# A recurrent mixer's convolution split between VectorE and GpSimd, with its two norms in the other order

## The chip, the cores and the metric

The kernel runs on one core of a Trainium2 chip. The metric is the device time of one execution in microseconds. Five engines take part: TensorE (PE, with its weight loads shown as PEld), VectorE (DVE), ScalarE (ACT), GpSimd (POOL) and SyncE (SP), which issues the loads.

## The reference

The program runs two model blocks one after the other on 512 tokens of width 1024. The part that matters here is the mixer of the first layer, `mixer_ab`: a recurrence over the tokens (RWKV-7, eight heads of 64) beside a causal depthwise convolution of 31 taps over 512 channels.

```python
y = rwkv7_scan(rh, hs(decay), kh, vh, kk, hs(a))
mu = jnp.mean(y, axis=-1, keepdims=True)                 # group norm: per head
yc = y - mu
y = yc * lax.rsqrt(jnp.mean(yc * yc, axis=-1, keepdims=True) + GN_EPS)
y = y.reshape(b, t, D_RWKV) * lnx_g + lnx_b
bonus = jnp.sum(rh * kh * r_k, axis=-1, keepdims=True) * vh
y_a = (y + bonus.reshape(b, t, D_RWKV)) * g
glu = c_val * jax.nn.sigmoid(c_gate)
conv = lax.conv_general_dilated(glu, conv_w[:, None, :], window_strides=(1,),
    padding=[(CONV_WIDTH - 1, 0)], dimension_numbers=('NWC', 'WIO', 'NWC'),
    feature_group_count=D_CONV) + conv_b                 # CONV_WIDTH = 31
y_b = jax.nn.silu(layer_norm(conv, conv_ln_g, conv_ln_b, CONV_LN_EPS))
return jnp.concatenate([y_a, y_b], axis=-1) @ w_out      # x = x + rms_norm(that, g[3])
```

All data is float32. Everything else (four plain feed-forward parts, an attention mixer, two hybrid mixers, two cross attentions, two gated feed-forward parts) is untouched by the change, apart from line numbers.

## The kernel before

Activations lie features by tokens: a tile is 128 features (partitions) by 512 tokens, so the mixer's output is 8 tiles: tiles 0 to 3 of `H` hold the recurrent half, tiles 4 to 7 the convolution half. Each large product splits both operands into a rounded part and a remainder and runs three matmuls for each pair of tiles (L245, L246, L254): ScalarE rounds (`WHI`, `WK_R`), VectorE subtracts (`WLO`, `H_LO`).

The code is one instruction stream for each engine, written out by hand; semaphores order the streams. Nothing is scheduled by a planner: an engine does its instructions in the order of its stream, and a wait holds everything behind it.

The mixer (`make_mixa`) runs like this. TensorE makes 22 panels of the input projection; VectorE scales each (L2507, L2509), shifts it (L2514) and makes the factors of the recurrence. `factors_made` counts these; it reaches 24 when `rho_made` (L2460) is done, and from then on the tiles of `e_in` are free, in whose place the convolution's sums `acc` lie. Then VectorE inverts 32 by 32 triangles (L2529, L2530: 31 steps of two small instructions, each waiting for the last), masks two Gram matrices out of PSUM (L2474, `masked`), and runs the convolution.

The convolution is 31 taps on 4 tiles. A tap is one VectorE instruction on a 128 by 512 tile, `acc = glu shifted by j * weight + acc` (L2490, with `glu` and `acc` both in SBUF; the first tap of a tile is a `tensor_scalar`, L2487). The list runs over all tiles for tap 0, then tap 1 and so on. `conv(n)` puts the next n of the 124 into VectorE's stream. They fill places where VectorE would wait:

- `conv(68)` ahead of the four additions into `rho` (L2537), which wait for TensorE's first four rounds of `tokens` (L2248);
- `conv(20)` ahead of the scan;
- `conv(1)` in each of the scan's 14 steps;
- `conv(6)` and the last 16 after the scan, between instructions of the group norm.

The scan goes over chunks of 32 tokens. In each step VectorE makes a decayed state `d` (L2544, L2545), takes one tap, and adds TensorE's product out of PSUM (L2551, two halves); TensorE then makes the next product (L2266) and the step's outputs (L2271).

After the scan ScalarE copies `y` out of PSUM (L2365). The group norm follows: sums by head (L2276), centring (L2554), squares (L2368), their sums (L2113), root and reciprocal (L2371, L2557), spread back to the tiles (L2120), then three VectorE instructions for each of 4 tiles (L2565 to L2567). The layer norm of the convolution needs all taps: sums over channels (L2285), centring (L2562), squares (L2374), sums (L2290), root (L2377), reciprocal (L2569), spread (L2295), product (L2572), SiLU (L2380). Then `parts_act` and `parts_dve` split the 8 tiles, 0 to 7, and the output product takes them in that order, tile by tile in its first panel.

GpSimd does almost nothing in the mixer: one DMA for the small weights and three memsets.

Of the kernel before, what the change touches and what calls it, by code (L numbers as in the profile page):

```python
# [27 lines left out]
ALU = mybir.AluOpType  # L28
# [6 lines left out]
T = 512  # L35
# [5 lines left out]
HD = 64  # L41
# [49 lines left out]
def build(nc, dram, out, phases, final=True):  # L91
    ctx = ExitStack()
    with ctx:
# [142 lines left out]
        def feature_hi(pe, p, s_, hi, ks, first, i=0, n=T, fresh=None):  # L236


            slot = p.nslot(s_)
            pe.wait_ge(S("w_lo"), p.N + (s_ + 1))  # L240
            for b_, k in enumerate(ks):
                w, o = slice(128 * b_, 128 * b_ + 128), PS[:, 4 * p.slot + i, 0:n]
                if fresh:
                    pe.wait_ge(S(fresh[0]), fresh[2] + k + 1)
                pe.matmul(o, WHI[:, slot, w], hi(k), start=(first and b_ == 0), stop=False)  # L245
                pe.matmul(o, WLO[:, slot, w], hi(k), start=False, stop=False)  # L246

        def feature_lo(pe, p, s_, lo, ks, last, i=0, n=T, fresh=None):

            for b_, k in enumerate(ks):  # L250
                w, o = slice(128 * b_, 128 * b_ + 128), PS[:, 4 * p.slot + i, 0:n]
                if fresh:
                    pe.wait_ge(S(fresh[1]), fresh[2] + k + 1)
                mm = pe.matmul(o, WHI[:, p.nslot(s_), w], lo(k), start=False, stop=(last and b_ == len(ks) - 1))  # L254
            mm.then_inc(S("piece_done"), 1)
# [1779 lines left out]
def make_mixa(env):  # L2035
# [31 lines left out]
    KKB, LORA = [1, 2, 3, 5], [6, 7]  # L2067

# [18 lines left out]
    def pool(pool, idx, n, b):  # L2087
        pool.wait_ge(S("norm_sum"), b["norm"] + 1)
        pool.dma_start(SC[:, 2:4, :], env["dram"]["a_lora"].rearrange("p (a c) -> p a c", a=2)).then_inc(S("lora_loaded"), 16)
        nc.gpsimd.memset(glu[:, :, 0:PAD], 0.0).then_inc(S("pool_set"), 1)  # L2090
        pool.wait_ge(S("glu_made"), 4)
        nc.gpsimd.memset(Tp, 0.0).then_inc(S("pool_set"), 1)
        pool.wait_ge(S("pool_set"), 2)
        nc.gpsimd.memset(flat(HID, 16, 1024)[:, 0:1024:C + 1], 1.0).then_inc(S("pool_set"), 1)

    def pe(pe, idx, n, b):
# [176 lines left out]

        for f in range(4):
            pe.wait_ge(S("y_copied"), f + 1)
            pe.matmul(PS[:, BA[f], :], blk, y[:, f, :], start=True, stop=True).then_inc(S("gn_sums"), 1)  # L2276
        for f in range(4):
            pe.wait_ge(S("head_squares"), 4 + f + 1)
            head_sums(f, BB[f], SC[:, 4:8, :], "gn_sums")
        pe.wait_ge(S("head_recips"), 2)  # L2280
        for f in range(4):
            head_spread(f, BA[f], "gn_sums")
        pe.wait_ge(S("conv_tap"), 4 * CONVW)
        for f in range(4):
            mm = pe.matmul(PS[:, BB[0], :], ones, acc[:, f, :], start=(f == 0), stop=(f == 3))  # L2285
        mm.then_inc(S("gn_sums"), 1)
        for f in range(4):
            pe.wait_ge(S("head_squares"), 8 + f + 1)
            for t in range(TT):
                mm = pe.matmul(PS[:, BB[1], 128 * t:128 * t + 128], csq[:, f, 128 * t:128 * t + 128], ones, start=(f == 0 and t == 0),  # L2290
                               stop=(f == 3 and t == TT - 1))
        mm.then_inc(S("gn_sums"), 1)
        pe.wait_ge(S("head_recips"), 3)
        for t in range(TT):
            mm = pe.matmul(PS[:, BB[2], 128 * t:128 * t + 128], recips[:, t:t + 1].to_broadcast([128, 128]), ident, start=True, stop=True)  # L2295
        mm.then_inc(S("gn_sums"), 1)

    def act(act, idx, n, b):
# [85 lines left out]
        env["parts_act"](act, made, b["mix"], DT, HI0)  # L2384

    def dve(dve, idx, n, b):
# [90 lines left out]
        taps = [(j, f) for j in range(CONVW) for f in range(4)]  # L2477
        done = [0]

        def conv(count):  # L2480

            for _ in range(min(count, len(taps) - done[0])):
# [5 lines left out]
                else:  # L2488
                    dve.wait_ge(S("conv_tap"), done[0] - 3)
# [44 lines left out]
        conv(68)  # L2534
# [3 lines left out]
        conv(20)  # L2538
        dve.wait_ge(S("ef_copied"), 16)
        for c in range(1, NCH - 1):  # L2540
# [7 lines left out]
            for par in range(2):  # L2548
                rows = slice(64 * par, 64 * par + 64)
                f_s = PS[rows, BA[2 * (c % 2) + par], 0:256].rearrange("p (h v) -> p h v", h=NHP)  # L2550
                tt(state(c + 1)[rows], d[rows], f_s, ALU.add).then_inc(S("state_ready"), 1)  # L2551
        for f in range(4):
            dve.wait_ge(S("gn_sums"), f + 1)
            stt(out=y[:, f, :], in0=PS[:, BA[f], :], scalar=-1.0 / HD, in1=y[:, f, :], op0=ALU.mult, op1=ALU.add).then_inc(S("centred"), 1)  # L2554
# [4 lines left out]
        dve.wait_ge(S("conv_tap"), 4 * CONVW)  # L2559
        dve.wait_ge(S("gn_sums"), 13)  # L2560
        for f in range(4):
            stt(out=acc[:, f, :], in0=PS[:, BB[0], :], scalar=-1.0 / 512, in1=acc[:, f, :], op0=ALU.mult, op1=ALU.add).then_inc(S("centred"), 1)  # L2562
        for f in range(4):
            dve.wait_ge(S("gn_sums"), 8 + f + 1)
            st.done(stt(out=y[:, f, :], in0=y[:, f, :], scalar=vec("lnx_g", f), in1=PS[:, BA[f], :], op0=ALU.mult, op1=ALU.mult))  # L2565
            st.done(stt(out=y[:, f, :], in0=y[:, f, :], scalar=vec("lnx_b", f), in1=bonus[:, f, :], op0=ALU.add, op1=ALU.add))
            tt(H[:, f, :], y[:, f, :], G_[:, f, :], ALU.mult).then_inc(S("rwkv_out"), 1)  # L2567
        dve.wait_ge(S("head_roots"), 6)
        ve.reciprocal(recips[:, 0:TT], sums[:, 0:TT]).then_inc(S("head_recips"), 1)  # L2569
        dve.wait_ge(S("gn_sums"), 15)  # L2570
        for f in range(4):
            tt(acc[:, f, :], acc[:, f, :], PS[:, BB[2], :], ALU.mult).then_inc(S("ln_normed"), 1)  # L2572
        env["parts_dve"](dve, b["mix"], DT, HI0)
# [129 lines left out]
```

## Time and profile before

| what | before |
|---|---|
| median of 3 runs | 3728.59 us (3719.97 to 3729.72) |
| the profiled execution | 3726.07 us, its span 3724.3 us |
| TensorE busy | 95% of the span |
| VectorE busy | 53% |
| ScalarE busy | 40% |
| GpSimd busy | 20.6 us, 1% |
| mean granted TensorE clock | 0.975 of full speed |

In the page's 40 slices of the span TensorE is busy nine tenths or more nearly everywhere, except in slices 6 to 8, about 560 to 750 us: the recurrence, its scan and the two norms. There TensorE's granted clock also falls. A stage bound by TensorE gives nothing when another engine gets faster; this stretch is where VectorE and the waits between the engines set the time. How the rows are read: a timeline row gives start, length, engine, line, operation, output and inputs with shapes, and in brackets the engine's idle time ahead of it with who ended it. A row of the chain of waits gives a piece of the path that ended last.

### The profile page before, as it was taken

What the parts mean: (1) busy time and instruction counts of PE and PEld (TensorE: products, weight loads), DVE (VectorE), ACT (ScalarE), POOL (GpSimd) and SP (SyncE); (2) the same over time, 40 slices, a digit from 0 to 9 for tenths busy, and PEclk for the clock granted to TensorE, in tenths of its full rate; (3) what the DMA queues carried; (4) which work ended last, traced back from release to release, by engine and by line L of the source; (5) the groups of instructions that cost most, each with busy time, mean ns of one, the idle gap of its engine ahead of it and who ended that gap; (6) DMA issues with size and microseconds to landing.
All of it is one profiled execution on the core that took longest, in us unless ns stands there. A gap on an engine that the chain in (4) does not pass through costs nothing.

```text
span 3724.3 us, 55194 instructions
## 1 busy us (share of the span) xinstructions
PE 3544.7 (95%) x21764; PEld 2954.4 (79%) x21764; DVE 1961.6 (53%) x2712; ACT 1473.7 (40%) x2212; POOL 20.6 (1%) x38
## 2 busy tenths in 40 slices
PE   7999996699999999999999999999999998989998
PEld 6888775578887888898678888778788896778887
DVE  3442469844434443325744433755677357566753
ACT  3332432143323332334643323655444237454432
POOL 0000000000000000000000000000000000000000
PEclk9999996699999999999999999999999999999999
DMA  3223220012232223222022233102222330222232
GB/s 114 96 94 99 78 69 15 2 63 96 96 95 81 96 97 95 85 91 85 7 79 96 96 94 95 38 29 86 91 96 94 99 101 13 68 80 90 96 94 92
DMA packets 84100, 296.11 MB, mean 80 GB/s; under 512 B 9504, under 2 KB 9504, under 8 KB 83680
## 3 DMA queue, kind: packets, MB, share of 16 engines
q1 hardware_dynamic: 82512, 288.24, 24.5%
q0 software_dynamic: 1424, 5.51, 0.4%
q8 instruction: 124, 2.03, 0.2%
q14 instruction: 40, 0.33, 0.0%
HBM read 291.61 MB, written 2.10 MB: 79 GB/s over the span
## 4 chain that ended last, share of the span: by engine, by line
PE 89%; DVE 6%; ACT 2%; issue 2%; DMA 1%; SPq 0%; DVEq 0%; ACTq 0%
PE PS L254 22%; PE PS L245 22%; PE PS L246 22%; PE PS L331 2%; PE PS L334 2%; PE PS L332 2%; PE PS L365 2%; PE PS L937 2%; PE PS L948 1%; PE PS L961 1%; PE PS L277 1%; DVE H_LO L438 1%; PE PS L278 1%; ACT WHI L217 1%; DVE WLO L221 1%
## 5 line engine op out<-in xcount | busy, mean ns | idle before, releaser
L245 PE MATMUL PS<-WK_R,WHI 128*128 128x512 f32 (+1 forms) x3680 | 1430.4, 389 | 13.6 <-ACT WK_R L585 6.9
L246 PE MATMUL PS<-WK_R,WLO 128*128 128x512 f32 (+1 forms) x3680 | 1425.5, 388 | 0.0
L221 DVE TENSOR_TENSOR WLO<-RAW,WHI 128x1024 fp32r<-128x1024 f32 x563 | 689.1, 1225 | 1211.9 <-ACT WHI L217 1209.2
L217 ACT ACTIVATE WHI<-RAW 128x1024 fp32r<-128x1024 f32 x563 | 596.0, 1059 | 995.0 <-PE PS L254 820.7
L245 PEld LDWEIGHTS PS<-WK_R,WHI 128*128 128x128 f32 x3680 | 692.8, 188 | 164.9 <-issue 19.6
L246 PEld LDWEIGHTS PS<-WK_R,WLO 128*128 128x128 f32 x3680 | 692.8, 188 | 141.0 <-issue 0.7
L254 PE MATMUL PS<-H_LO,WHI 128*128 128x512 f32 x2680 | 674.4, 391 | 4.7 <-DVE H_LO L438 4.3
L254 PEld LDWEIGHTS PS<-H_LO,WHI 128*128 128x128 f32 x2680 | 501.9, 188 | 118.6 <-DVE H_LO L438 16.4
L254 PE MATMUL PS<-HID_LO,WHI 128*128 128x512 f32 x1056 | 263.2, 389 | 0.0
L254 PEld LDWEIGHTS PS<-HID_LO,WHI 128*128 128x128 f32 x1056 | 197.9, 188 | 40.9
L1129 DVE SCALAR_TENSOR_TENSOR SC<-SC,VEC 128x511 f32<-128x511 f32 x176 | 132.2, 751 | 110.5 <-ACT SC L1096 98.6
L331 PE MATMUL PS<-WHI,WK_R 128*128 128x256 f32 (+1 forms) x608 | 159.2, 293 | 1.6 <-DVE WLO L221 1.6
L613 ACT ACTIVATE WK_R<-HID (+1 forms) x88 | 55.6, 632 | 260.9 <-DVE HID L630 260.9
L332 PE MATMUL PS<-WLO,WK_R 128*128 128x256 f32 (+1 forms) x608 | 158.8, 292 | 0.0
L1096 ACT ACTIVATE SC<-SC,VEC 128x512 f32<-128x512 f32 x88 | 71.8, 816 | 178.9 <-DVE SC L1119 178.9
L610 ACT ACTIVATE SC<-SC 128x512 f32<-128x512 f32 x88 | 55.7, 632 | 159.4 <-DVE SC L624 158.9
L331 PEld LDWEIGHTS PS<-WHI,WK_R 128*128 128x128 f32 x608 | 115.9, 191 | 2.1 <-issue 1.8
L332 PEld LDWEIGHTS PS<-WLO,WK_R 128*128 128x128 f32 x608 | 116.0, 191 | 0.0
L632 DVE TENSOR_TENSOR HID_LO<-HID,WK_R (+1 forms) x88 | 60.9, 693 | 86.7 <-ACT WK_R L613 86.7
L1010 DVE TENSOR_REDUCE AS<-PS 128x2 f32<-128x1024 f32 (+2 forms) x80 | 85.1, 1064 | 32.6 <-PE PS L937 31.1
L365 PEld LDWEIGHTS PS<-CON,SC 128*128 128x128 f32 x640 | 82.4, 193 | 17.8 <-ACT SC L515 6.7
L365 PE MATMUL PS<-CON,SC 128*128 128x128 f32 x640 | 86.0, 279 | 7.8 <-ACT SC L515 4.1
(375 smaller groups left out, 3526.0 us busy)
## 6 DMA issues: line engine op xcount, KB each, us to landing
RAW<-in_ffn_gu SPq DMA_DIRECT2D x176, 512.0 KB, 3.5
RAW<-in_f_up SPq DMA_DIRECT2D x88, 512.0 KB, 3.6
RAW<-in_ffn_dn SPq DMA_DIRECT2D x64, 512.0 KB, 3.5
RAW<-in_c_in SPq DMA_DIRECT2D x32, 512.0 KB, 3.5
RAW<-in_f_dn SPq DMA_DIRECT2D x32, 512.0 KB, 3.5
RAW<-in_ffn_dn SPq DMA_DIRECT2D x32, 384.0 KB, 3.1
RAW<-in_a_in SPq DMA_DIRECT2D x22, 512.0 KB, 3.4
RAW<-in_b_out SPq DMA_DIRECT2D x16, 512.0 KB, 3.6
```

The source lines that it names most:

```text
L217: nc.scalar.activation(WHI[:, slot, :], RAW[:, slot, :], ACT.Copy).then_inc(S("w_hi"), 1)
L221: nc.vector.tensor_tensor(WLO[:, slot, :], RAW[:, slot, :], WHI[:, slot, :].bitcast(F32), ALU.subtract).then_inc(S("w_lo"), 1)
L245: pe.matmul(o, WHI[:, slot, w], hi(k), start=(first and b_ == 0), stop=False)
L246: pe.matmul(o, WLO[:, slot, w], hi(k), start=False, stop=False)
L254: mm = pe.matmul(o, WHI[:, p.nslot(s_), w], lo(k), start=False, stop=(last and b_ == len(ks) - 1))
L331: pe.matmul(o, hi(k, t), WHI[:, slot, w], start=(first and b_ == 0), stop=False)
L332: pe.matmul(o, hi(k, t), WLO[:, slot, w], start=False, stop=False)
L334: mm = pe.matmul(o, lo(k, t), WHI[:, slot, w], start=False, stop=(last and b_ == len(ks) - 1))
L365: mm = pe.matmul(PS[:, b_, 128 * t:128 * t + 128], SC[:, k, 128 * t:128 * t + 128], ones, start=(first and t == 0), stop=(last and t == TT ...
L937: mm = pe.matmul(PS[:, score_banks(u).start + i, 0:n], q, k_, start=(k == 0), stop=(k == len(products) - 1))
L1010: nc.vector.reduce_max(stat(1, U), PS[:, banks, 0:n], AX.X, negate=True).then_inc(S("at_max"), 1)
L1129: nc.vector.scalar_tensor_tensor(out=o, in0=s, scalar=vec("fcw", (idx * 3 + tap) * 2 * FT + part * FT + e), in1=o, op0=ALU.mult, op1=ALU.a ...
```

## The change

It has four parts, all in the mixer or in helpers that only the mixer uses differently.

1. **GpSimd makes tile 3 of the convolution.** Once `factors_made` reaches 24, it runs 31 taps as two instructions each: a product of the shifted `glu` with the weight (broadcast along the tokens) into a spare tile `WK[:, 29]`, and an addition to `acc[:, 3]`. Each waits for the one before by the semaphore `conv_pool`: 62 instructions of 128 by 512, all inputs in SBUF.
2. **VectorE's 93 taps** (3 tiles) all stand ahead of the scan: `conv(62)` ahead of the additions into `rho`, `conv(31)` behind them. The `conv(1)` in the scan's steps finds nothing left.
3. **Layer norm ahead of group norm.** Behind the scan TensorE sums `acc` over channels first, then the head sums of `y`, and so on; the two norms alternate. Banks of PSUM are dealt out anew for that.
4. **Output tiles in the order 4 to 7, 0 to 3.** ScalarE and VectorE split the convolution half first, and the output product takes its tiles in that order (in each of its 8 panels).

The core of the diff:

```diff
@@ feature_hi, feature_lo
-                w, o = slice(128 * b_, 128 * b_ + 128), PS[:, 4 * p.slot + i, 0:n]
+                w, o = slice(128 * (k % 8), 128 * (k % 8) + 128), PS[:, 4 * p.slot + i, 0:n]
@@ out_pieces
+            if kind == "mixa":
+                return [[4, 5, 6, 7, 0, 1, 2, 3]]
@@ make_mixa
+    OUT_ORDER = (4, 5, 6, 7, 0, 1, 2, 3)
+    OWN = 3
+    SPREAD = [BA[1], BA[2], BA[3], BB[3]]
@@ pool
+        pool.wait_ge(S("factors_made"), 24)
+        part, o = WK[:, 29, :], acc[:, OWN, :]
+        for j in range(CONVW):
+            w = vec("cw", 4 * j + OWN).to_broadcast([128, T])
+            if j > 0:
+                pool.wait_ge(S("conv_pool"), 2 * j)
+            nc.gpsimd.tensor_tensor(part, glu[:, OWN, j:j + T], w, ALU.mult).then_inc(S("conv_pool"), 1)
+            pool.wait_ge(S("conv_pool"), 2 * j + 1)
+            before = vec("cb", OWN).to_broadcast([128, T]) if j == 0 else o
+            nc.gpsimd.tensor_tensor(o, part, before, ALU.add).then_inc(S("conv_pool"), 1)
@@ pe, behind the scan
+        pe.wait_ge(S("conv_tap"), 3 * CONVW)
+        pe.wait_ge(S("conv_pool"), 2 * CONVW)
+        for f in range(4):
+            mm = pe.matmul(PS[:, BA[0], :], ones, acc[:, f, :], start=(f == 0), stop=(f == 3))
+        mm.then_inc(S("ln_sums"), 1)
...
+        pe.wait_ge(S("ln_recip"), 1)
...
         pe.wait_ge(S("head_recips"), 2)
         for f in range(4):
-            head_spread(f, BA[f], "gn_sums")
-        pe.wait_ge(S("conv_tap"), 4 * CONVW)
...
+            head_spread(f, SPREAD[f], "gn_sums")
@@ dve
-        taps = [(j, f) for j in range(CONVW) for f in range(4)]
+        taps = [(j, f) for j in range(CONVW) for f in range(OWN)]
...
-        conv(68)
+        conv(62)
...
-        conv(20)
+        conv(31)
...
-        conv(6)
+        dve.wait_ge(S("ln_root"), 1)
+        ve.reciprocal(recips[:, 0:TT], sums[:, 0:TT]).then_inc(S("ln_recip"), 1)
+        dve.wait_ge(S("ln_sums"), 3)
+        for f in range(4):
+            tt(acc[:, f, :], acc[:, f, :], PS[:, BA[0], :], ALU.mult).then_inc(S("ln_normed"), 1)
         dve.wait_ge(S("head_roots"), 5)
         ve.reciprocal(recips, sums).then_inc(S("head_recips"), 1)
-        conv(len(taps))
...
```

How the streams change at the places the prediction speaks of. VectorE from the end of the inverse into the scan, before (L2490 is a tap, L2537 the additions into `rho`, L2551 the state):

```order
L2531 STREAM_TRANSPOSE SC<-HID 128x32x32
L2474 TENSOR_TENSOR HID<-PS,CON 128x512 x4
L2487 TENSOR_SCALAR WK<-WK,VEC 128x512 x4
L2490 SCALAR_TENSOR_TENSOR WK<-WK,VEC 128x512 x64
L2537 TENSOR_TENSOR HID<-HID,PS 128x512 x4
L2490 SCALAR_TENSOR_TENSOR WK<-WK,VEC 128x512 x20
L2544 TENSOR_TENSOR RS<-H,ST 128x256
L2545 TENSOR_TENSOR RS<-RS,H 128x256
L2490 SCALAR_TENSOR_TENSOR WK<-WK,VEC 128x512
L2551 TENSOR_TENSOR WK<-RS,PS 64x256 x2
```

VectorE at the same place in the changed kernel (L2506 is a tap, L2553 the additions, L2567 the state):

```order
L2547 STREAM_TRANSPOSE SC<-HID 128x32x32
L2490 TENSOR_TENSOR HID<-PS,CON 128x512 x4
L2503 TENSOR_SCALAR WK<-WK,VEC 128x512 x3
L2506 SCALAR_TENSOR_TENSOR WK<-WK,VEC 128x512 x59
L2553 TENSOR_TENSOR HID<-HID,PS 128x512 x4
L2506 SCALAR_TENSOR_TENSOR WK<-WK,VEC 128x512 x31
L2560 TENSOR_TENSOR RS<-H,ST 128x256
L2561 TENSOR_TENSOR RS<-RS,H 128x256
L2567 TENSOR_TENSOR WK<-RS,PS 64x256 x2
```

Six fewer taps ahead of the additions, eleven more behind them, none between the scan's instructions.

TensorE behind the scan, before (L2276, L2113, L2120 group norm; L2285, L2290, L2295 layer norm; L245 the output product):

```order
L2271 MATMUL PS<-HID 64x32 x16
L2276 MATMUL PS<-WK,CON 128x512 x4
L2113 MATMUL PS<-CON,SC 128x128 x16
L2120 MATMUL PS<-CON,ST 64x128 x32
L2285 MATMUL PS<-WK,CON 128x512 x4
L2290 MATMUL PS<-CON,WK 128x128 x16
L2295 MATMUL PS<-CON,ST 128x128 x4
```

And in the changed kernel (L2292, L2300, L2308 layer norm; L2296, L2128, L2135 group norm):

```order
L2286 MATMUL PS<-HID 64x32 x16
L2292 MATMUL PS<-WK,CON 128x512 x4
L2296 MATMUL PS<-WK,CON 128x512 x4
L2300 MATMUL PS<-CON,WK 128x128 x16
L2128 MATMUL PS<-CON,SC 128x128 x16
L2308 MATMUL PS<-CON,ST 128x128 x4
L2135 MATMUL PS<-CON,ST 64x128 x32
```

Each step of the layer norm now stands ahead of a step of the group norm; the instructions are the same in number and kind.

GpSimd in the changed kernel, behind its last memset of the mixer (the pair L2106, L2109 comes 31 times):

```order
L2099 MEMSET HID 128x32 [waits pool_set]
L2106 ISA
L2106 TENSOR_TENSOR WK<-WK,VEC 128x512 [waits factors_made]
L2109 TENSOR_TENSOR WK<-WK,VEC 128x512 [waits conv_pool]
L2106 TENSOR_TENSOR WK<-WK,VEC 128x512 [waits conv_pool]
L2109 TENSOR_TENSOR WK<-WK 128x512 [waits conv_pool]
```

GpSimd's next instruction before the change, the loads of the first hybrid mixer, comes more than a millisecond later.

## Rows read from the trace of the kernel before

**Rows 1.** The page's first line.

```profile
span 3724.3 us, 55194 instructions
```

**Rows 2.** Timeline of VectorE, 575 to 703 us: start, length, engine, line, operation.

```profile
575.13 0.19 DVE L2529 TENSOR_TENSOR RS<-SC,HID 128x31 f32<-128x31 f32 x1
...
604.51 42.49 DVE L2490 SCALAR_TENSOR_TENSOR WK<-WK,VEC 128x512 f32<-128x512 f32 x64
649.61 2.48 DVE L2537 TENSOR_TENSOR HID<-HID,PS 128x512 f32<-128x512 f32 x4 [2.61 <-PE PS L2248]
...
668.34 0.87 DVE L2551 TENSOR_TENSOR WK<-RS,PS 64x256 f32<-64x256 f32 x2 [1.41 <-PE PS L2266]
669.24 0.42 DVE L2544 TENSOR_TENSOR RS<-WK,ST 128x256 f32<-128x256 f32 x1
...
702.22 0.87 DVE L2551 TENSOR_TENSOR HID<-RS,PS 64x256 f32<-64x256 f32 x2
```

**Rows 3.** Timeline of TensorE, the scan's first two products.

```profile
667.17 1.12 PE L2266 MATMUL PS<-H,WK 64*64 64x64 f32 x16
...
669.26 1.12 PE L2266 MATMUL PS<-WK 64*64 64x64 f32 x16 [0.17 <-DVE WK L2551]
```

**Rows 4.** Chain of waits, 703 to 751 us: start, length, piece.

```profile
704.91 6.66 PE PS L2276 x8
...
716.52 10.52 DVE WK L2490 x16
...
735.49 0.67 DVE WK L2565
...
747.15 2.93 ACT H L2380 x4
...
750.74 0.77 PE PS L245
```

**Rows 5.** Timeline of TensorE, sums and spreads of the two norms.

```profile
716.57 3.71 PE L2120 MATMUL PS<-CON,ST 128*64 128x128 f32 x64 [1.45 <-DVE ST L2557]
...
734.41 3.84 PE L2290 MATMUL PS<-CON,WK 128*128 128x128 f32 x32 [1.52 <-ACT WK L2374]
744.31 2.07 PE L2295 MATMUL PS<-CON,ST 128*128 128x128 f32 x8 [6.06 <-DVE ST L2569]
```

**Rows 6.** Timeline of ScalarE: rounding the mixer's output; first panel done.

```profile
749.98 4.25 ACT L585 ACTIVATE WK_R<-H 128x512 fp32r<-128x512 f32 x8
758.60 0.60 ACT L515 ACTIVATE SC<-PS 128x512 f32<-128x512 f32 x1 [4.37 <-PE PS L254]
```

**Rows 7.** Busy time by stretch: window, length, then by engine; PEclk is the granted clock.

```profile
751.00:755.20 4.20, 4.20 (x11) 3.24 (x11) 4.20 (x8) 3.23 (x7) 0.00 (x0) 0.50 0.02 4
```

**Rows 8.** Timeline of GpSimd, one of its six additions (in a hybrid mixer).

```profile
2427.43 1.27 POOL L1645 TENSOR_TENSOR HID<-HID 128x512 f32<-128x512 f32 x1 [135.85 <-ACT HID L1883]
```

**Rows 9.** Timeline of VectorE around that addition, and one round later.

```profile
2426.75 1.22 DVE L1010 TENSOR_REDUCE AS<-PS 128x2 f32<-128x1024 f32 x1
...
2428.08 1.30 DVE L1019 TENSOR_SCALAR SC<-SC,AS 128x512 f32<-128x512 f32 x2
...
2433.54 1.22 DVE L1010 TENSOR_REDUCE AS<-PS 128x2 f32<-128x1024 f32 x1 [1.27 <-PE PS L937]
...
2434.87 0.88 DVE L1019 TENSOR_SCALAR SC<-SC,AS 128x512 f32<-128x512 f32 x2
```

**Rows 10.** Timelines of VectorE and TensorE, 549 to 568 us.

```profile
549.90 2.49 DVE L2460 TENSOR_TENSOR HID<-HID,WK 128x512 f32<-128x512 f32 x4
...
557.06 1.23 DVE L221 TENSOR_TENSOR WLO<-RAW,WHI 128x1024 fp32r<-128x1024 f32 x1 [4.02 <-ACT WHI L217]
...
562.50 1.22 DVE L221 TENSOR_TENSOR WLO<-RAW,WHI 128x1024 fp32r<-128x1024 f32 x1 [0.54 <-ACT WHI L217]
...
567.45 2.65 PE L2133 MATMUL PS<-WK,HID 64*32 64x32 f32 x186 [6.13 <-DVE HID L2514]
```

**Rows 11.** Busy time by stretch, VectorE alone: the small instructions of the inverse.

```profile
575.10:598.50 23.40, 21.27 (x62) 0.72 0.02 4
```

More of the change, by code:

```diff
@@ L2272, in pe @@
         mm.then_inc(S("y_done"), 1)
+        pe.wait_ge(S("conv_tap"), 3 * CONVW)
[3 more added lines that the diff above has]
+        mm.then_inc(S("ln_sums"), 1)
         for f in range(4):
             pe.wait_ge(S("y_copied"), f + 1)
-            pe.matmul(PS[:, BA[f], :], blk, y[:, f, :], start=True, stop=True).then_inc(S("gn_sums"), 1)
+            pe.matmul(PS[:, BB[f], :], blk, y[:, f, :], start=True, stop=True).then_inc(S("gn_sums"), 1)
+        for f in range(4):
+            pe.wait_ge(S("ln_squares"), f + 1)
+            for t in range(TT):
+                mm = pe.matmul(PS[:, BA[1], 128 * t:128 * t + 128], csq[:, f, 128 * t:128 * t + 128], ones, start=(f == 0 and t == 0),
+                               stop=(f == 3 and t == TT - 1))
+        mm.then_inc(S("ln_sums"), 1)
         for f in range(4):
@@ L2279, in pe @@
             head_sums(f, BB[f], SC[:, 4:8, :], "gn_sums")
+        pe.wait_ge(S("ln_recip"), 1)
+        for t in range(TT):
+            mm = pe.matmul(PS[:, BA[0], 128 * t:128 * t + 128], recips[:, t:t + 1].to_broadcast([128, 128]), ident, start=True, stop=True)
+        mm.then_inc(S("ln_sums"), 1)
         pe.wait_ge(S("head_recips"), 2)
         for f in range(4):
-            head_spread(f, BA[f], "gn_sums")
-        pe.wait_ge(S("conv_tap"), 4 * CONVW)
[L2284 to L2296, printed above, removed]
+            head_spread(f, SPREAD[f], "gn_sums")
     def act(act, idx, n, b):
@@ L2366, in act @@
         for f in range(4):
+            act.wait_ge(S("ln_centred"), f + 1)
+            sc.activation(csq[:, f, :], acc[:, f, :], ACT.Square).then_inc(S("ln_squares"), 1)
+        for f in range(4):
             act.wait_ge(S("centred"), f + 1)
             sc.activation(SC[:, 4 + f, :], y[:, f, :], ACT.Square).then_inc(S("head_squares"), 1)
+        act.wait_ge(S("ln_sums"), 2)
+        sc.activation(sums[:, 0:TT], PS[:, BA[1], 0:T:128], ACT.Sqrt, bias=eps[:, 3:4], scale=1.0 / 512).then_inc(S("ln_root"), 1)
+        act.wait_ge(S("ln_recip"), 1)
         for f in range(4):
@@ L2488, in conv @@
                 else:
-                    dve.wait_ge(S("conv_tap"), done[0] - 3)
+                    dve.wait_ge(S("conv_tap"), done[0] - 2)
                     i = stt(out=acc[:, f, :], in0=src, scalar=w, in1=acc[:, f, :], op0=ALU.mult, op1=ALU.add)
@@ L2551, in dve @@
                 tt(state(c + 1)[rows], d[rows], f_s, ALU.add).then_inc(S("state_ready"), 1)
+        assert done[0] == len(taps)
+        dve.wait_ge(S("ln_sums"), 1)
+        dve.wait_ge(S("conv_tap"), len(taps))
+        dve.wait_ge(S("conv_pool"), 2 * CONVW)
+        for f in range(4):
+            stt(out=acc[:, f, :], in0=PS[:, BA[0], :], scalar=-1.0 / 512, in1=acc[:, f, :], op0=ALU.mult, op1=ALU.add).then_inc(S("ln_centred"), 1)
         for f in range(4):
             dve.wait_ge(S("gn_sums"), f + 1)
-            stt(out=y[:, f, :], in0=PS[:, BA[f], :], scalar=-1.0 / HD, in1=y[:, f, :], op0=ALU.mult, op1=ALU.add).then_inc(S("centred"), 1)
@@ L2559, in dve @@
[L2559 to L2562, printed above, removed]
         for f in range(4):
             dve.wait_ge(S("gn_sums"), 8 + f + 1)
-            st.done(stt(out=y[:, f, :], in0=y[:, f, :], scalar=vec("lnx_g", f), in1=PS[:, BA[f], :], op0=ALU.mult, op1=ALU.mult))
+            st.done(stt(out=y[:, f, :], in0=y[:, f, :], scalar=vec("lnx_g", f), in1=PS[:, SPREAD[f], :], op0=ALU.mult, op1=ALU.mult))
```

33 lines of the change are left out of this document (12 added, 21 removed).

## The prediction

> **What bounds the kernel now.** I read the page first: the profiled execution spans 3724.3 us [rows 1] of its 3726.1, and TensorE is busy in 95% of it. Only the mixer of the first layer, some 190 us, is not TensorE's. There I read the timelines of VectorE and TensorE side by side, then the chain of waits. What the reader is to see:
>
> Ahead of the scan both engines are close to level. VectorE's 64 taps take 42.49 us, 0.664 each; then it waits 2.61 us for TensorE before the additions into `rho`, which end at 652.1 [rows 2]. At the scan's first state it waits 1.41 us for TensorE.
>
> In the scan VectorE is the bound: its states come from 668.34 to 702.22, 13 periods of 2.606 us, without a gap [rows 2]. The one period in which TensorE had the last word is the first: from product to product 2.09 us [rows 3]. So a tap costs the scan about 0.52 us a step.
>
> Behind the scan everything hangs in one chain: head sums, centring, group norm's sums, 16 taps in a row (10.52 us), the layer norm's sums, the twelve instructions of the group norm (from 735.49, about 8.7 us), spread, SiLU, and only then TensorE's output product at 750.74 [rows 4]. Its first panel is done at 758.6 [rows 6]. From the last state (703.1) that is 55.5 us.
>
> **The change, part by part.** All times are set against the profiled execution's 3726.1 us, 2.5 below the median.
>
> *Taps ahead of the scan.* 3 tensor_scalars and 59 taps are shorter than what stood there, so without any disturbance the `rho` additions still wait for TensorE and end at 652.1. Behind them stand 31 taps: 31 x 0.664 = 20.6, to 672.7, plus two small ones (0.46 each): the first state comes at 673.6, not 668.3: **+5.3 us**.
>
> *The scan.* 13 periods of 2.09 for 2.606 [rows 2, 3]: **-6.7 us**. Its last state is then ready at 701.7: 1.4 us earlier in all. What is late next in the scan is TensorE's product.
>
> *Behind the scan.* Call the last state's end 0. Before, the first output panel is done at 55.5. Now:
> - The layer norm's sums need no copy of `y` and start at about 1.1; four products of 128 by 512 took 6.66 at the low clock [rows 4]: 7.8.
> - The head sums of `y` follow directly. The engine has then been busy without a break, and in the profile the sums behind a busy stretch run faster; bounds 3.3 (half of 6.66, twice the clock) and 6.66, I take 4: 11.8.
> - Sums of the layer norm's squares, 3.8: 15.6. Sums of the group norm's squares, as many matmuls of the same size, 3.7: 19.3 [rows 5]. ScalarE's and VectorE's parts run beside them.
> - The layer norm's spread, 1 to 2.1 [rows 5], say 1.6: 20.9. Its four products on VectorE 2.5 (as four instructions with one PSUM input in [rows 2]): 23.4; SiLU (2.93, [rows 4]) and rounding are beside that.
> - The group norm's reciprocal stands behind these four; its spread takes 3.7 [rows 5]. VectorE's twelve instructions begin after a quarter of it, about 24.7, and last 8.7: 33.4. TensorE starts the output product at about 27.4 with tiles 4 to 7 and then waits for tiles 0 to 3.
> - Eight remainders `H_LO` of about 0.61 on VectorE stand behind the twelve: 38.3. They were hidden before (VectorE idle during SiLU) and are now last: TensorE's third part follows them. Panel done at 38.5.
>
> So **-17.0 us**. The output product's start at the low clock (0.50 in its first 4.2 us, [rows 7]) was paid before as well; broken up as it now is, it may be paid again in the second panel: 0 to +2.2, I take **+1.9**.
>
> Sum of these: 5.3 - 6.7 - 17.0 + 1.9 = -16.5, that is 3709.6, if GpSimd's 62 instructions cost nobody anything.
>
> *GpSimd's instructions.* An addition of 128 by 512 takes 1.27 us [rows 8]. They start when `rho_made` is done, 552.3 [rows 10]; 62 x about 1.33 = 82 us, to 635, far ahead of the scan's end. So GpSimd's own time is hidden, as long as nobody disturbs it.
>
> *Whom they disturb.* Two rows decide here. While GpSimd's addition ran (from 2427.43), VectorE issued a pair of tensor_scalars, SBUF to SBUF, at 2428.08, and they took 1.30 us; the same pair one round later took 0.88 [rows 9]. All four places in the trace where the two meet look like this. So VectorE was held 0.42 us, until 1.07 us after GpSimd's start. The reduction out of PSUM that also overlapped took the usual 1.22 [rows 9]. I read this as: a running GpSimd tensor_tensor keeps something of SBUF's for about 1.07 us of its 1.27, and VectorE's SBUF work waits for it whole. No row shows a VectorE instruction with two SBUF inputs beside GpSimd. The bounds are no hold at all (as for the PSUM reader) and a hold by the whole of GpSimd's instruction. I take the hold of 1.07, since a tap and the inverse's instructions take both inputs from SBUF and write to it, and are thus nearer to the tensor_scalar than to the reduction.
>
> Then each of GpSimd's 62 instructions costs VectorE 1.07 less the 0.15 or so of its own instruction that needs no data (a tap of 0.664 has 512 columns; the inverse's smallest, 31 columns, still takes 0.19, [rows 2]): 0.9 each, **56 us**. Where do they fall? From 552.3 on: the two splits of weights, `kappa_made`, `kappa_end_made` and two shifts, twelve instructions with two SBUF inputs, on whose end TensorE already waits 6.13 us [rows 10]; then the inverse, 62 dependent instructions in 23.4 us [rows 11], on which `tokens` and so everything depends. VectorE has idle time of 4.0 and 0.5 us there [rows 10], two waits more behind, and some instructions out of PSUM, which are not held: I take off 9, by estimate. Remains **+47 us**, all on the path, since nothing else that TensorE has by then fills the time. By the time VectorE reaches its taps, GpSimd has ended. Bounds: if the product with a broadcast weight holds only half as long, 31 x 0.9 + 31 x 0.35 - 9 = +30; if the hold is the whole 1.27, 62 x 1.1 - 9 = +59.
>
> The sum: 3726.1 - 16.5 + 47 = 3756.6. I say **3756 us**, own range 3738 to 3770.
>
> A page bears on this. The Trainium skill, "SBUF — State Buffer", section "Who interferes with whom", says that VectorE and GpSimd share one pair of SBUF ports, that a VectorE instruction with two SBUF inputs contends with a GpSimd instruction that reads SBUF, and that whichever comes first holds the pair for its whole length. By that rule the change comes out near the forecast, and without it near 3710. The trace's held tensor_scalars agree with the page's lock for one kind of instruction (0.42 us of delay); for two inputs no run here shows it.
>
> **The rivals.**
>
> *No hold for two-input instructions.* VectorE's taps and inverse run as before beside GpSimd. For it: the trace holds no row against it, only the tensor_scalar was held, which may use SBUF in another way than a scalar_tensor_tensor. Against it: both inputs must come out of SBUF. Price: the sum without the +47, **3709 us** (3705 to 3714). Faster.
>
> *VectorE goes first and GpSimd starves.* If a busy VectorE wins each time, GpSimd gets only VectorE's idle and PSUM time: some 7 instructions by 575, 4 around the transposes and masks (598.5 to 604.5), 3 at the `rho` additions, 1 in each of 14 steps, 28 to 30 in all at the scan's end. 32 x 1.33 = 43 us remain, and TensorE's stream has the wait for `conv_pool` ahead of everything behind the scan, the head sums of `y` too. The layer norm's sums then start near 746 and the panel is done 37.4 later, 783 for 758.6: +25, with the clock term 3751 to 3753; **3751 us**. For it: VectorE's instructions follow each other without a gap. Against it: in [rows 9] it was VectorE that waited. It becomes a loss as soon as more than 18 us of GpSimd's work remain at the scan's end.
>
> *Shared, not held.* Both engines slow each other in part; half of 47: +23, **3733 us**, within what can be told from no change or just above.
>
> **How the numbers follow.** A measurement of this kernel tells about 0.3% (11 us) from no change. Forecast, VectorE held: 0.48. GpSimd starved: 0.13. Shared: 0.12, of which 0.02 come out slower by more than that. No hold: 0.27. So slower 0.63, within 0.3% 0.10, faster 0.27. The case on the other side holds more than 2 in 10, so the range must reach it: 3706 to 3770. Of this the forecast's own part is 3738 to 3770.
>
> **What would show it.** Held: the inverse's 62 instructions, 23.4 us before, take about 60, each of the larger ones 1.3 us start to start; the two splits and shifts around 560 are stretched; GpSimd ends its 62nd near 640, and the scan starts some 50 us later than before. No hold: the inverse still takes 23.4 and the first state comes at 673.6. Starved: GpSimd's instructions lie far apart during the taps, and TensorE stands idle behind the scan on `conv_pool`. For the rest: states every 2.09 us; taps of 0.664 ahead of the scan; the output product starting 27 us behind the last state and its first panel done at 38, with `H_LO` as the last wait. The prediction is wrong if a GpSimd product with a broadcast operand takes much longer than 1.27 us, if the hold covers less than the overlap I read, or if VectorE's two-input instructions do not ask for what GpSimd keeps.

## The result: 20 us slower, and the profile after

The changed kernel takes 3748.8 us (median, 3748.1 to 3749.1), the kernel before 3728.1 in the same comparison: 1.006 times as long, 95% interval 1.0042 to 1.0077. The forecast was 3756, slower. The profiled execution spans 3747.2 us, against 3724.3 [rows 1].

Times of the two traces are compared from the end of the last `rho_made` on, which comes at 552.3 before and at 550.0 after; these 2.3 us lie ahead of everything that was changed and are added below where it says "late".

**GpSimd and the inverse.** Two timelines of the changed kernel: start, length, engine, line, operation. First GpSimd (L2106 the product, L2109 the addition), with the end of its 62 instructions:

```profile
592.47 1.04 POOL L2106 TENSOR_TENSOR WK<-WK,VEC 128x512 f32<-128x512 f32 x1
593.58 1.27 POOL L2109 TENSOR_TENSOR WK<-WK 128x512 f32<-128x512 f32 x1
594.93 1.04 POOL L2106 TENSOR_TENSOR WK<-WK,VEC 128x512 f32<-128x512 f32 x1
...
631.61 1.30 POOL L2109 TENSOR_TENSOR WK<-WK 128x512 f32<-128x512 f32 x1
```

And VectorE in the inverse over the same time (L2545 and L2546 are the two instructions of a step):

```profile
592.58 1.10 DVE L2545 TENSOR_TENSOR RS<-SC,HID 128x156 f32<-128x156 f32 x1
593.71 1.32 DVE L2546 TENSOR_TENSOR HID<-HID,RS 128x156 f32<-128x156 f32 x1
595.06 1.10 DVE L2545 TENSOR_TENSOR RS<-SC,HID 128x175 f32<-128x175 f32 x1
...
631.82 1.34 DVE L2546 TENSOR_TENSOR HID<-HID,RS 128x231 f32<-128x231 f32 x1
633.20 0.39 DVE L2545 TENSOR_TENSOR RS<-SC,HID 128x220 f32<-128x220 f32 x1
```

The reader is to see a lockstep. VectorE's instructions start about 0.1 us behind GpSimd's and end just behind them, 1.10 to 1.14 beside the short one, 1.31 to 1.37 beside the long one, for every width from 87 to 256 columns. GpSimd sets the pace here and loses little: its own two take 1.10 and 1.32 beside the widest, 1.04 and 1.27 beside the narrow ones. With GpSimd's last instruction gone (632.9) the same kind takes 0.39. The costs by group (busy us, mean ns, in 550 to 640 us), after:

```profile
L2546 DVE TENSOR_TENSOR HID<-HID,RS 128x31 f32<-128x31 f32 (+15 forms) x31 | 30.1, 970 | 1.1
L2545 DVE TENSOR_TENSOR RS<-SC,HID 128x31 f32<-128x31 f32 (+15 forms) x31 | 25.9, 837 | 1.1
```

Together 56.0 us, for the 21.27 of [rows 11]: 34.7 more, while 41 of GpSimd's instructions ran, **0.85 each**.

**Ahead of the inverse**, VectorE's timeline again (what stood there before is in [rows 10]; L2467 and L2480 are `kappa`'s instructions, L2530 the shift, L2523 and L2537 read PSUM):

```profile
554.78 1.57 DVE L221 TENSOR_TENSOR WLO<-RAW,WHI 128x1024 fp32r<-128x1024 f32 x1 [4.02 <-ACT WHI L217]
...
563.97 2.28 DVE L221 TENSOR_TENSOR WLO<-RAW,WHI 128x1024 fp32r<-128x1024 f32 x1
566.18 0.68 DVE L2523 TENSOR_TENSOR SC<-PS,RS 128x512 f32<-128x512 f32 x1
566.78 5.70 DVE L2467 TENSOR_TENSOR SC<-HID,ST 128x512 f32<-128x512 f32 x4
572.40 1.52 DVE L2530 SCALAR_TENSOR_TENSOR HID<-SC,VEC,HID 128x511 f32<-128x511 f32 x1
573.95 2.48 DVE L2537 TENSOR_TENSOR WK<-HID,PS 128x512 f32<-128x512 f32 x4
...
579.76 1.98 DVE L2540 STREAM_TRANSPOSE SC<-HID 128x1024 f32<-128x1024 f32 x1
581.77 0.73 DVE L2545 TENSOR_TENSOR RS<-SC,HID 128x31 f32<-128x31 f32 x1
```

The first split takes 1.57 for 1.23, the second 2.28 for 1.22, each four of `kappa` 5.7 (2.5 in the trace of before), a shift 1.52 (0.74): all have two inputs in SBUF. The readers of PSUM (0.68; 2.48 for four) and the transpose (1.98) take what they took. The inverse begins 8.9 us late.

**What became of the lateness.** TensorE waits for the masked matrices, first row; then VectorE's stream up to the scan:

```profile
644.27 5.89 PE L2220 MATMUL PS<-H,SC 32*32 32x64 f32 x249 [34.15 <-DVE HID L2490]
```

```profile
645.40 39.18 DVE L2506 SCALAR_TENSOR_TENSOR WK<-WK,VEC 128x512 f32<-128x512 f32 x59
687.01 2.48 DVE L2553 TENSOR_TENSOR HID<-HID,PS 128x512 f32<-128x512 f32 x4 [2.43 <-PE PS L2263]
689.41 20.62 DVE L2506 SCALAR_TENSOR_TENSOR WK<-WK,VEC 128x512 f32<-128x512 f32 x31
...
710.87 0.87 DVE L2567 TENSOR_TENSOR WK<-RS,PS 64x256 f32<-64x256 f32 x2
...
713.02 0.87 DVE L2567 TENSOR_TENSOR WK<-RS,PS 64x256 f32<-64x256 f32 x2 [0.37 <-PE PS L2281]
...
738.94 0.87 DVE L2567 TENSOR_TENSOR HID<-RS,PS 64x256 f32<-64x256 f32 x2 [0.37 <-PE PS L2281]
```

The masks are done at 644.1, 43.7 late. The taps run at 0.664, since GpSimd has ended. The additions wait for TensorE as before [rows 2], 39.7 late: TensorE's stretch from the masks to them took 42.9 us instead of 46.8, at a granted clock of 0.66 instead of 0.63. The first state is 44.8 late, the last (738.94) 39.0: a step is 2.16 us, in which VectorE waits 0.37 for TensorE.

**Behind the scan**, TensorE's timeline, then the two rows of VectorE and ScalarE that end the first output panel:

```profile
740.86 5.41 PE L2292 MATMUL PS<-WK,CON 128*128 128x512 f32 x8
746.10 3.60 PE L2296 MATMUL PS<-WK,CON 128*128 128x512 f32 x8
749.54 3.73 PE L2300 MATMUL PS<-CON,WK 128*128 128x128 f32 x32
753.11 3.74 PE L2128 MATMUL PS<-CON,SC 128*128 128x128 f32 x32
756.68 1.06 PE L2308 MATMUL PS<-CON,ST 128*128 128x128 f32 x8
760.57 5.38 PE L2135 MATMUL PS<-CON,ST 128*64 128x128 f32 x64 [2.83 <-DVE ST L2583]
```

```profile
770.54 4.90 DVE L592 TENSOR_TENSOR H_LO<-H,WK_R 128x512 fp32r<-128x512 f32 x8
```

```profile
776.02 0.60 ACT L517 ACTIVATE SC<-PS 128x512 f32<-128x512 f32 x1 [4.74 <-PE PS L254]
```

From the last state's end (739.81) to the panel 36.2 us, for 55.5 [rows 4 and 6]. So the panel is 19.7 late: 39.0 less 19.3. The median moved by 20.7.

### The profile page after: what moved, and what is told of

It reads as the page before. It is cut to its first block, busy times and chain, and to the rows that moved or that the text cites. A ratio compares the mean times of both kernels' runs of the same rounds, so it can differ in the third digit from the quotient of the medians.

```text
span 3747.2 us, 55226 instructions
## 1 busy us (share of the span) xinstructions
PE 3540.8 (94%) x21764; PEld 2952.5 (79%) x21764; DVE 1983.4 (53%) x2681; ACT 1474.6 (39%) x2212; POOL 98.7 (3%) x100
## 4 chain that ended last, share of the span: by engine, by line
PE 73%; DVE 7%; ACT 2%; issue 2%; DMA 1%; DVEq 0%; ACTq 0%; SPq 0%
PE PS L254 18%; PE PS L245 17%; PE PS L246 17%; PE PS L331 2%; PE PS L332 2%; PE PS L334 2%; PE PS L939 2%; PE PS L365 1%; PE PS L950 1%; PE PS L963 1%; DVE HID L2546 1%; DVE WLO L221 1%; DVE RS L2545 1%; DVE H_LO L438 1%; ACT WHI L217 1%
## 5 line engine op out<-in xcount | busy, mean ns | idle before, releaser
L245 PE MATMUL PS<-WK_R,WHI 128*128 128x512 f32 (+1 forms) x3680 | 1429.4, 389 | 10.9 <-DVE WLO L221 4.7
L245 PEld LDWEIGHTS PS<-WK_R,WHI 128*128 128x128 f32 x3680 | 691.8, 188 | 162.6 <-issue 15.5
L254 PE MATMUL PS<-H_LO,WHI 128*128 128x512 f32 x2680 | 676.2, 392 | 4.8 <-DVE H_LO L438 4.4
L254 PEld LDWEIGHTS PS<-H_LO,WHI 128*128 128x128 f32 x2680 | 502.6, 188 | 120.0 <-DVE H_LO L438 16.4
L254 PE MATMUL PS<-HID_LO,WHI 128*128 128x512 f32 x1056 | 263.2, 389 | 0.0
L254 PEld LDWEIGHTS PS<-HID_LO,WHI 128*128 128x128 f32 x1056 | 197.9, 188 | 41.0
```

## The experiments

Each run is compared with the kernel before on its own chip (median given with it). "The panel" is the first output panel of the mixer, its lateness counted as above.

**Does the price hang on GpSimd at all?** The tile's instructions go, all else stays.

```diff
@@ pool
-        part, o = WK[:, 29, :], acc[:, OWN, :]
-        for j in range(CONVW):
...
+        nc.gpsimd.memset(acc[:, OWN, :], 0.0).then_inc(S("conv_pool"), 1)
```

> The changed kernel without GpSimd's 62 instructions: tile 3 of the convolution is left out (one memset of its sums stands in its place), all else stays. Theory (GpSimd's tensor_tensors hold VectorE's instructions with two SBUF inputs, one for one): the inverse's 62 instructions take 23.4 us again instead of 58, the 43.6 us of lateness at the masks vanish and the time falls to about 3705 (3748.8 less 43.6), below the kernel before by some 23. Rival (the lateness comes from something else in the change, such as the new places of the taps or the order of the instructions): the inverse stays long and the time stays near 3748.

3705.1 us (before 3721.8), ratio 0.9956 [0.9941, 0.9971]. The changed kernel's ratio is 1.006, so the 62 instructions cost 0.0104 of 3728, **39 us** (the two intervals together allow 30 to 47), and everything else gains 16.4 (11 to 22; the prediction had 16.5). The panel is 22.3 us early, so that between the two traces the tile costs 42.0 there. The inverse takes its old 23.4 us, and the additions into `rho` wait 4.16 us for TensorE.

**What of GpSimd holds VectorE: writing, one input, or two?** In place of the tile, 124 memsets of a spare tile (write alone), or 62 products with a constant (one input).

```diff
@@ pool
+        for j in range(124):
+            pool.wait_ge(S("conv_pool"), j + 1)
+            nc.gpsimd.memset(WK[:, 29, :], 0.0).then_inc(S("conv_pool"), 1)
```

```diff
@@ pool
+        for j in range(62):
+            pool.wait_ge(S("conv_pool"), j + 1)
+            nc.gpsimd.tensor_scalar(out=WK[:, 29, :], in0=glu[:, OWN, j // 2:j // 2 + T], scalar1=0.5, scalar2=None, op0=ALU.mult).then_inc(S("conv_pool"), 1)
```

> As e1, tile 3 of the convolution left out, but GpSimd runs 124 memsets of 128 by 512 one after the other from the same point on, about 70 to 80 us of work that only writes SBUF. Theory (what is held is SBUF's read side): nothing is slowed, the inverse takes 23.4 us, the time is that of e1, about 3705. Rival (any GpSimd instruction on SBUF holds VectorE, the write side too): the inverse takes 50 us or more and the time is 3730 to 3750.

> GpSimd's 62 instructions are replaced by 62 products with a constant, 128 by 512, each with ONE input in SBUF and its output in SBUF, one after the other in the same place of the program; the sum of tile 3 of the convolution is left out (it stays zero). Reading as such holds VectorE: each of the 62 holds VectorE's two-input instructions as an addition does, the inverse takes 45 to 60 us instead of 23.4, the time is 3730 to 3748 us. Only a GpSimd instruction with TWO inputs holds: the inverse takes 23.4 us as with writes alone, the 62 end whenever they like, and the time is that without the tile, 3703 to 3707 us. A hold shorter than for two inputs would show as an inverse between the two with VectorE's starts in step with GpSimd's.

Memsets: 3703.3 (before 3721.8), ratio 0.9952 [0.9936, 0.9967], as without the tile. GpSimd's row shows them back to back across the whole inverse, which takes 23.4 us as before. Behind it stand the rows of VectorE's three tensor_scalars, the first taps, which have one input in SBUF: beside the memsets, and in the kernel without the tile:

```profile
551.70 72.72 POOL L2104 MEMSET WK<- 128x512 f32 x124
```

```profile
601.45 2.12 DVE L2498 TENSOR_SCALAR WK<-WK,VEC 128x512 f32<-128x512 f32 x3
```

```profile
601.11 1.43 DVE L2495 TENSOR_SCALAR WK<-WK,VEC 128x512 f32<-128x512 f32 x3
```

So writing alone does not hold VectorE's instructions with two inputs, but it does hold these: 2.12 us for 1.43. The prediction read its hold on a pair of tensor_scalars [rows 9]; that is another case than the one it needed.

One input: 3717.5 (before 3726.2), ratio 0.9981 [0.9971, 0.9991]: 0.0025 or 9 us (3 to 16) above the kernel without the tile. Neither theory in pure form: a third, short hold. GpSimd's row (by group), then VectorE in the inverse:

```profile
L2104 POOL TENSOR_SCALAR WK<-WK 128x512 f32<-128x512 f32 x62 | 98.1, 1581 | 5.1
```

```profile
589.49 0.42 DVE L2541 TENSOR_TENSOR HID<-HID,RS 128x256 f32<-128x256 f32 x1
589.95 0.42 DVE L2540 TENSOR_TENSOR RS<-SC,HID 128x255 f32<-128x255 f32 x1
590.41 0.71 DVE L2541 TENSOR_TENSOR HID<-HID,RS 128x255 f32<-128x255 f32 x1
591.15 0.42 DVE L2540 TENSOR_TENSOR RS<-SC,HID 128x252 f32<-128x252 f32 x1
```

About once in each 1.6 us one VectorE instruction takes 0.29 more; the others slip in beside GpSimd's. The inverse takes 28.8 us instead of 23.4, and the 59 taps behind it, still beside GpSimd, 48.3 instead of 39.2. This run changes three things at once, the number of inputs, the kind of instruction (tensor_scalar for tensor_tensor) and its length (1.58 us); that the number of inputs is what shortens the hold is likely, but not shown.

**Is the price in proportion?** Only 30 of the 62 instructions; 16 taps of tile 3 are left out.

```diff
@@ pool
-        for j in range(CONVW):
+        for j in range(15):
```

> The changed kernel with GpSimd's first 30 instructions alone (15 taps of tile 3; its other 16 taps are left out). Theory (a price for each instruction): about 19 of them fall ahead of the inverse (8.9 us of lateness there, as in the changed kernel) and 11 into it at 0.81 us each: masks about 18 us late and the time about 3723, that is 18 above the kernel without GpSimd's instructions. Rival (a price for GpSimd's being busy at all, or for its start): nearly all of the 43.6 us or nearly none.

3728.0 (before 3725.6), ratio 1.0005 [0.9996, 1.0014], by the ratios 18 us above the kernel without the tile, as expected, for 39 with all 62. (That the time itself is 5 above the 3723 I gave is mostly this chip, on which the kernel before takes 3.8 more.) In the trace the masks are 16.9 late after 30 instructions, 43.7 after 62: some 21 of them fall ahead of the inverse, where they leave it about 9 late, and the other nine lengthen the inverse by 7.9, 0.88 each.

**Would it be cheaper beside the taps?** GpSimd starts when the masks are done, so that the inverse is spared.

```diff
@@ pool
         pool.wait_ge(S("factors_made"), 24)
+        pool.wait_ge(S("mats_masked"), 8)
```

> The changed kernel with one wait more: GpSimd starts only when the inverse and the masks behind it are done, so that its 62 instructions run beside VectorE's taps. Theory (each GpSimd instruction holds any VectorE instruction with two SBUF inputs, wherever): the inverse takes 23.4 us, but the taps ahead of the additions into rho come every 1.5 to 1.6 us instead of 0.664; the additions are some 50 us late and the time is 3750 to 3760, no better than the changed kernel. Rival (only the inverse's chain of dependent small instructions suffers, while taps that don't wait for each other slip in between): additions into rho less than 15 us late, time 3705 to 3725, faster than the kernel before.

3756.2 (before 3725.6), ratio 1.009 [1.0075, 1.0106]: the slowest of all. VectorE's row and three of GpSimd's:

```profile
602.99 91.87 DVE L2507 SCALAR_TENSOR_TENSOR WK<-WK,VEC 128x512 f32<-128x512 f32 x59
```

```profile
621.32 1.36 POOL L2107 TENSOR_TENSOR WK<-WK,VEC 128x512 f32<-128x512 f32 x1
622.76 1.61 POOL L2110 TENSOR_TENSOR WK<-WK 128x512 f32<-128x512 f32 x1
624.44 1.37 POOL L2107 TENSOR_TENSOR WK<-WK,VEC 128x512 f32<-128x512 f32 x1
```

A tap takes 1.56 us for 0.664, 0.89 more, and GpSimd's own two take 1.36 and 1.6 for 1.04 and 1.27. Each engine waits for the other's instruction, one by one, though not for all of it: 1.56 is less than 0.664 and GpSimd's mean of 1.155 together (1.82), so about a quarter of a microsecond of the two overlaps. VectorE does not starve GpSimd, which ends at 696.0. This is the rival with starvation, tried where VectorE has the longest unbroken run, and it falls. It also shows that 0.89 holds for a tap as 0.85 does for the inverse's small instructions: the inverse is no special victim.

**What do the other three parts bring?** All 124 taps on VectorE (68 and 56 ahead of the scan), with norms and output order as changed; then the same with output tiles 0 to 7.

```diff
@@ dve
-        conv(62)
+        conv(68)
...
-        conv(31)
+        conv(56)
```

```diff
@@ out_pieces, and OUT_ORDER in make_mixa
-            if kind == "mixa":
-                return [[4, 5, 6, 7, 0, 1, 2, 3]]
```

> The changed kernel with all four tiles on VectorE: 68 taps ahead of the additions into rho, 56 behind them, GpSimd idle, the new order of the norms and of the output tiles kept. Theory: the inverse takes 23.4; the first state comes 56 x 0.664 + 0.9 = 38.1 us behind the additions, some 22 later than in the kernel before; the scan gives back 5.8 (2.16 a step for 2.606) and the stretch behind it 19.3, as in the changed kernel: about 3 us less than before, 3725, that is 24 less than the changed kernel. Rival (the stretch behind the scan is short only because little was left late by GpSimd): 3735 or more.

> The kernel of e3 (all tiles on VectorE, 68 and 56 taps ahead of the scan, layer norm first), but with the output tiles split and multiplied in the order 0 to 7. Theory (the last wait of the first output panel is VectorE's eight remainders behind the group norm's twelve instructions, whatever the order): the first panel is done at most 2 us later than in e3 (36.2 us behind the last state there), the time 3721 to 3725 on this chip. Rival (the order is what hides the group norm's end): 5 us or more later, 3727 and above.

3721.6 (before 3721.8), ratio 0.9999 [0.9989, 1.0008], where I had expected 3 us less than before, which the interval allows; with the old order 3724.5 (before 3725.6), ratio 1.0002 [0.9992, 1.0011]. Against the kernel without the tile, tile 3 on VectorE costs 3721.6 - 3705.1 = 16.5 us: 25 taps more behind the additions, 25 x 0.664 = 16.6. On GpSimd it costs 39. From the centring of the layer norm to the panel it is 29.9 us with the new order and 31.5 with the old one, so the order of output tiles is worth 1.6 us in the trace, less than the medians resolve. From the last state on it is 36.2 and 38.7, more than the 2 us that I had allowed; the other 1.0 lies in the layer norm's sums, from their start to the next row's (5.04 and 6.03 us), which the order does not touch.

**A version with the taps in VectorE's own waits.** All taps on VectorE, the new norms and order, but 7 taps in the wait of 4.02 us at the first split [rows 10], 3 between the masks of the two Gram matrices, 70 ahead of the `rho` additions, 30 behind, one in each scan step.

```diff
@@ dve
+                if kind == 1 and par == 0:
+                    conv(3)
...
+            if i == 19:
+                dve.wait_ge(S("factors_made"), 24)
+                conv(7)
...
-        conv(62)
+        conv(70)
...
-        conv(31)
+        conv(30)
```

> All four tiles on VectorE, new order of norms and output tiles, but taps in places where VectorE waits: 7 in its wait of 4.0 us behind the shift of the 20th panel, 3 between the two masks where it waits 2.0 us, 70 ahead of the additions into rho, 30 behind them, 14 in the scan. Theory: first state 30 x 0.664 + 0.9 = 20.8 us behind the additions (16.2 before): +4.6; scan unchanged at 2.606 a step; -19.3 behind the scan: -14.7, about 3713, faster than both. Rival (the taps in the early waits delay the splits of weights and with them TensorE): 3718 to 3725.

3711.5 (before 3721.8), ratio 0.9974 [0.9962, 0.9985]: 10 us (6 to 14) faster than the kernel before, where I had expected 14.7; with the next one the fastest version that computes everything. The panel is 14.1 early. VectorE's additions into `rho` have no wait left:

```profile
601.22 46.44 DVE L2497 SCALAR_TENSOR_TENSOR WK<-WK,VEC 128x512 f32<-128x512 f32 x70
647.58 2.47 DVE L2547 TENSOR_TENSOR HID<-HID,PS 128x512 f32<-128x512 f32 x4
```

**Eight of its taps behind the scan**, beside the head sums of `y`, which then come first.

```diff
@@ dve
-        conv(30)
+        conv(22)
...
+        conv(8)
```

> The kernel of e4, with 8 of the 30 taps ahead of the scan moved behind it, into VectorE's wait of 7.3 us there, and for that the head sums of y ahead of the layer norm's sums (centring and squares in the same order); the rest of the layer norm stays ahead. Theory: the first state comes 8 x 0.664 = 5.3 us earlier, the stretch behind the scan grows by less than 1 us: about 5 us below e4, 3706 to 3708 on a chip where e4 takes 3711.5, about 0.4% faster than the kernel before. Rival (the layer norm's sums, now second, push back the whole tail by their 3.6 us or more): within 2 us of e4.

3714.2 (before 3725.6), ratio 0.9974 [0.9965, 0.9983], the same ratio, as the rival said and not the theory. The scan ends 5.3 us earlier and the tail takes 40.4 us instead of 36.9. TensorE's rows show where most of the 3.5 us go: the head sums wait for ScalarE's copy of `y` and start 1.8 us behind the last state where the layer norm's sums started at 1.05, these four products take 6.57 to the next row instead of 6.03, and TensorE waits 1.45 for the layer norm's squares.

```profile
701.99 6.72 PE L2281 MATMUL PS<-WK,CON 128*128 128x512 f32 x8 [0.70 <-ACT WK L2370]
708.56 3.60 PE L2284 MATMUL PS<-WK,CON 128*128 128x512 f32 x8
713.60 3.84 PE L2289 MATMUL PS<-CON,WK 128*128 128x128 f32 x32 [1.45 <-ACT WK L2376]
```

## Why the prediction was nearly right

The sign, the mechanism and the case held; of 28 us forecast 20.7 came (16 to 29 by the interval). By its steps, from the two profiled executions, and with the kernel without the tile where it isolates a step:

| step | predicted | measured |
|---|---|---|
| GpSimd's holds, up to the masks | +47 | +43.7 |
| TensorE from the masks to `rho` | 0 | -4.0 |
| taps behind the additions, first state | +5.3 | +5.1 |
| scan | -6.7 | -5.8 |
| behind the scan | -17.0 | -19.3 |
| low clock paid again | +1.9 | 0 |
| sum | +30.5 | +19.7 |

The measured sum is the lateness of the first output panel; the prediction placed its 1.9 behind that panel. All misses but the scan's have one sign, and they add up to 10.8 us.

**The holds.** The reading of [rows 8 and 9] carried over to instructions with two SBUF inputs, in part by luck: the memsets hold tensor_scalars and leave those with two inputs alone, so the row on tensor_scalars did not vouch for the others, as the rival "no hold" had said. The Trainium skill's rule for them ("SBUF — State Buffer", "Who interferes with whom": a shared pair of ports, held by whichever comes first for its whole length) agrees with the turns taken above, except that a quarter of a microsecond of each pair overlaps in the late start. Its condition on GpSimd, that it reads SBUF, agrees with the memsets. The size: I had 0.9 for each of the 62 with 9 off. In the inverse 41 instructions cost 34.7 us, where the same working gives 41 x 0.9 = 37; ahead of it 21 left the stream 8.9 us late, where it gives 21 x 0.9 - 9 = 10. So the term was 3.3 us too large. The mis-sized step is the price of one hold, 1.07 less 0.15 for every instruction alike. Beside the addition VectorE is held to its end and pays 1.00 (1.32 for 0.32, 156 columns), beside the product 0.78 (1.10 for 0.32): the first was taken too low and the second too high, and 0.9 came near the mean by two errors. Ahead of the inverse VectorE's twelve instructions with two SBUF inputs took 9.4 us longer, 0.8 each, of which the wait of 0.54 at the second split absorbed its part; how many of GpSimd's 21 fell on idle time or on readers of PSUM was an estimate that came out. The prediction took the product with a broadcast weight for an addition of 1.27; it takes 1.04, and GpSimd ended at 632.9 and not near 640. The bound "half the hold" for it was not needed: VectorE waits it out as it does the addition, 1.10 beside the one and 1.32 beside the other.

**TensorE's stretch** from the masks to `rho` had no term in the sum: the prediction held that nothing else fills the time. The 46.8 us became 42.9. TensorE's rows at the masks, before and after (L2197 and L2212 are the same product, the last ahead of the masked matrices):

```profile
598.57 3.67 PE L2197 MATMUL PS<-WK,HID 32*32 32x64 f32 x249 [0.78 <-ACT H L2351]
```

```profile
604.83 3.67 PE L2212 MATMUL PS<-WK,HID 32*32 32x64 f32 x249 [0.78 <-ACT H L2367]
```

Before, this product was not over when the masks were done (602.8; the last 7 of its matmuls start at 603.7), and TensorE began on the masked matrices 1.1 us behind them; in the changed kernel it was over long before 644.1, and TensorE began 0.14 us behind them. So one of the 4 us is work that did fill the wait. The other three are open. The granted clock rose from 0.63 to 0.66, which fits, but in the kernel without the tile the stretch took 44.6 at 0.68: longer than 42.9 at a higher clock.

**The scan.** 2.09 was read from one period, the first [rows 3], in which TensorE waited 0.17 us for the state. In all periods of the changed scan it waits 0.24 and the step is 2.16: 13 x 0.07 = 0.9 us, the whole miss. One period was too few to read a step from.

**Behind the scan.** The order of events was as written: the eight remainders last, from 770.54, and TensorE's third part following them. What was mis-sized is the clock of the first four products: 5.24 us to the next row's start instead of 6.66 (granted clock 0.72 in 741 to 747 us), and 3.60 for the head sums instead of 4. From there to the panel I had 26.7 us, and it took 26.5. The low clock did come once more (0.59 in 771.3 to 775.5 us, eight L254 in 3.87 instead of 1.98), but beside the remainders of the first panel, not in the second, which follows after 5.48 us (the later ones after 5.44); the +1.9 was wrong.

**The rivals.** "No hold" is refuted by the lockstep; its price was sound: 16.5 us below the kernel before was forecast, and the kernel without the tile is 16.7 below. "GpSimd starves" is refuted by the late start. "Shared, not held": both engines do slow each other, but VectorE pays for nearly the whole of GpSimd's instruction; 3733 would have needed half the price. Nearest to it comes the run with one input.

**What stays open.** Where three of the 4 us in TensorE's stretch went, and how much of what is gained or lost at the panel reaches the end. Without the tile the panel is 22.3 us early and its profiled span 22.8 shorter (3701.5), though the median fell by 16.7 only; in the changed kernel it is 19.7 late and the span 22.9 longer; with all taps on VectorE it is 5.6 early and the span 0.8 longer, with half the instructions 5.2 and 1.5 shorter, with the new places 14.1 and 12.2 shorter. The traces come from several chips and there is one of the kernel before, whose own times on one chip lie between 3722.2 and 3728.2; so single traces do not show a difference of a few us behind the panel, and whether an earlier panel costs something there was not tried.

## What to carry to other kernels

Before work is given to GpSimd beside a busy VectorE, price what it takes from VectorE, not what it takes itself: here a tap cost GpSimd two instructions, each of which held VectorE 0.85 to 0.89 us, 1.7 together, and relieved it of 0.664. That loses wherever VectorE's instructions have two inputs in SBUF and lie on the path, small dependent ones and taps alike. GpSimd's memsets could stand beside these, and VectorE's readers of PSUM beside GpSimd's additions. The same taps put into waits that VectorE had anyway gained 10 us.

## What the runs showed of the hardware

- VectorE's instruction with two SBUF inputs and GpSimd's tensor_tensor take turns, one for one: 1.10 to 1.14 beside the product and 1.31 to 1.37 beside the addition, for widths from 87 to 256 that alone take 0.25 to 0.43; as taps, 1.56 for 0.664, and GpSimd 1.36 and 1.6.
- GpSimd's memsets (0.59 us each) do not hold VectorE's instructions with two SBUF inputs, but they do hold its tensor_scalars from SBUF to SBUF (2.12 us for three instead of 1.43). A GpSimd tensor_scalar with one SBUF input (1.58 us) costs a stream with two inputs 0.29 us each; a tensor_tensor with two 0.85.
- VectorE's readers of PSUM (0.68) and its stream transpose (1.98) are not held by a running tensor_tensor.
- On GpSimd the product with an operand broadcast along the tokens takes 1.04 us, the addition of two full tiles 1.27.
